# A two-layer decoder trunk on one core: the second tile's shared up projection and the shared down products move to the middle of each layer's experts, and the third pair's down weights move into two dead buffers

## The reference

```
for layer in range(2):
    mix = even_mixer(...) if layer == 0 else odd_mixer(...)
    x = layer_norm(alpha * x + mix, ln1_g, ln1_b)
    ff = moe_ffn(x, ...)          # 64 routed experts + 1 shared expert
    x = layer_norm(alpha * x + ff, ln2_g, ln2_b)
```

## Time and profile before

| what | us |
|---|---|
| median of 3 runs (1289.89 to 1291.04) | 1290.01 |
| the profiled execution's own time | 1290.57 |
| its span | 1288.8 |
| TensorE busy in it | 1216.6 |
| layer 0's first up product of the experts starts | 201.9 |
| layer 0's last combine ends | 668.2 |
| layer 1's first up product of the experts starts | 809.3 |
| core's end | 1288.8 |

### The profile page before, as it was taken

How to read it: one execution, slowest core, us unless ns; L and a number is a source line. 1 busy time by engine, 2 the same in 40 slices (tenths; PEclk the granted TensorE clock), 3 DMA queues, 4 the chain that set the end, 5 groups by cost and what they waited for, 6 DMA issues and landing times.

```text
span 1288.8 us, 16653 instructions
## 1 busy us (share of the span) xinstructions
PE 1216.6 (94%) x6664; PEld 576.4 (45%) x6664; DVE 401.3 (31%) x884; ACT 299.2 (23%) x649; POOL 27.9 (2%) x97
## 2 busy tenths in 40 slices
PE   8999999999999989899979999999999998999995
PEld 5777854334343433333336665443434333343331
DVE  3667274212121221212133646321212212121214
ACT  3354322222121211111121343121112111111112
POOL 1004000000000000000010000000000000000000
PEclk9999999999999999999989999999999999999998
DMA  9317049899999999999992646699999999999992
GB/s 369 154 34 303 1 163 392 330 395 427 429 429 427 429 430 427 428 430 426 427 382 101 261 196 248 274 358 398 427 428 429 429 428 429 428 428 429 428 427 108
DMA packets 44716, 447.42 MB, mean 347 GB/s; under 512 B 8064, under 2 KB 9472, under 8 KB 18816
## 3 DMA queue, kind: packets, MB, share of 16 engines
q1 hardware_dynamic: 44080, 446.29, 83.3%
q10 hardware_dynamic: 592, 0.53, 0.2%
HBM read 445.75 MB, written 1.05 MB: 347 GB/s over the span
## 4 chain that ended last, share of the span: by engine, by line
PE 76%; DMA 16%; DVE 5%; ACT 2%; issue 1%; DVEq 0%; SPq 0%; ACTq 0%
PE psum L404 28%; DMA w_up_ring<-in_moe_up 15%; PE psum L509 13%; PE psum L420 4%; PE psum L2246 4%; PE psum L2101 4%; PE psum L1214 3%; PE psum L490 3%; PE psum L1664 2%; PE psum L604 2%; PE psum L469 2%; PE psum L638 1%; DVE moe_h L1061 1%; PE psum L1502 1%; PE psum L2252 1%
## 5 line engine op out<-in xcount | busy, mean ns | idle before, releaser
L404 PE MATMUL psum<-w_up_ring,moe_x_selected 128*64 128x512 f32 x2048 | 454.9, 594 | 20.4 <-DMA w_up_ring<-in_moe_up 20.4
L404 PEld LDWEIGHTS psum<-w_up_ring,moe_x_selected 128*64 128x64 f32 x2048 | 149.5, 137 | 314.8 <-issue 275.8
L509 PE MATMUL psum<-w_down_ring,moe_hT 128*64 128x512 f32 x992 | 226.5, 598 | 0.0
L1061 DVE SCALAR_TENSOR_TENSOR moe_h<-moe_silu,moe_slot_gate,psum 128x256 f32<-128x256 f32 x64 | 30.7, 480 | 406.8 <-ACT moe_silu L818 406.6
L818 ACT ACTIVATE moe_silu<-psum 128x256 f32<-128x256 f32 x64 | 24.6, 384 | 446.5 <-PE psum L404 446.5
L509 PEld LDWEIGHTS psum<-w_down_ring,moe_hT 128*64 128x64 f32 x992 | 68.1, 136 | 122.8 <-issue 108.8
L1066 DVE TENSOR_TENSOR moe_out_low<-psum,moe_out_high 128x512 fp32r<-128x512 f32 x64 | 44.3, 692 | 220.2 <-ACT moe_out_high L830 220.2
L830 ACT CAST moe_out_high<-psum 128x512 fp32r<-128x512 f32 x64 | 37.4, 585 | 125.2 <-PE psum L509 125.2
L1068 DVE TENSOR_TENSOR moe_out_low<-psum,moe_out_high 128x512 fp32r<-128x512 f32 x64 | 44.3, 692 | 65.6 <-ACT moe_out_high L832 65.6
L490 PE MATMUL psum<-moe_out_high,moe_matchT 32*128 32x512 f32 x496 | 62.4, 494 | 1.8 <-DVE moe_out_low L1068 1.8
L2101 PE MATMUL psum<-w_up_ring,mixed_transposed 128*128 128x512 f32 x128 | 56.5, 593 | 0.7 <-ACT mixed_transposed L1894 0.7
(11 more groups left out here) (499 smaller groups left out, 1069.1 us busy)
## 6 DMA issues: line engine op xcount, KB each, us to landing
w_up_ring<-in_moe_up SPq DMA_DIRECT2D x128, 2048.0 KB, 20.9
w_down_ring<-in_moe_down SPq DMA_DIRECT2D x62, 2048.0 KB, 20.7
w_up_ring<-in_ev_columns SPq DMA_DIRECT2D x4, 2048.0 KB, 15.4
w_up_ring<-in_od_w_in SPq DMA_DIRECT2D x4, 2048.0 KB, 15.1
w_up_ring<-in_ev_out SPq DMA_DIRECT2D x2, 2048.0 KB, 7.7
moe_shared_weights<-in_shared_up SPq DMA_DIRECT2D x2, 2048.0 KB, 7.7
w_up_ring<-in_od_w_out SPq DMA_DIRECT2D x2, 2048.0 KB, 7.8
ln_gain_bias<-in_ln_g SPq DMA_DIRECT2D x4, 512.0 KB, 9.3
```

The source lines that it names most:

```text
L404: last = nc.tensor.matmul(k.psum[e * SLOTS:(e + 1) * SLOTS, 6, :], xsel[:, kk, own:own + SLOTS], up_view(par, e, kk), start=kk == 0, stop= ...
L509: last = nc.tensor.matmul(k.psum[e * SLOTS:(e + 1) * SLOTS, bank, :], hT[:, j * P + e * SLOTS:j * P + (e + 1) * SLOTS], places[e][:, j, ha ...
L1061: nc.vector.scalar_tensor_tensor(h[:], silu[:], slot_gate[:, i:i + 1], up_ps[:, FE:2 * FE], ALU.mult, ALU.mult).then_inc(s.h, 1)
```

## The change

For each layer:

- The shared up weights get a place of their own below `SHARED_OFFSET` (where `w_down_extra` was), so nothing overwrites them. In layer 1 they are loaded by the odd mixer's loads, where the extra down weights were.
- Tile 1's `shared_up` leaves `first_two_pairs` and stands in quad 3, ahead of pair i = 1, with its output in bank 5. The four transposes stand ahead of i = 2.
- The four pieces of `shared_down` leave quad 7 and stand in quad 4, one ahead of each pair.
- Quads 3 and 4 are written out, between two loops (quads 1 and 2, quads 5 and 6).
- Pair 2's down weights go, in two loads of 1 MB, into `k.ln` (behind the norm) and `k.x` (behind the transposes and the low part). The ln2 tables are loaded later, behind pair 2's down product, and `k.x` is rebuilt by two additions on VectorE ahead of quad 7.

The diff, cut to its core:

```diff
@@ -44,6 +44,7 @@
+SHARED_UP, SHARED_DOWN = 3, 4
@@ -325,7 +326,7 @@
-    shared_w = at("shared_weights", [P, 2, KD, FE], F32, SHARED_OFFSET)
+    shared_w = mixer.shared_w if layer else at("shared_weights", [P, 2, KD, FE], F32, SHARED_OFFSET - 8 * KF * D)
@@ -364,12 +365,16 @@
-    extra_down_both = mixer.extra_down if layer else at("w_down_extra", [P, 2, KF, D], F32, SHARED_OFFSET - 8 * KF * D)
-    extra_down = [extra_down_both[:, i] for i in range(2)]
+    third_down = [k.ln[:], k.x[:]]
...
+    shared_bank = (1, 5)
+
+    def peeled(q, quad):
+
+        return isinstance(q, int) and q == quad
@@ -519,23 +524,23 @@
     def sync(sp):
         mixer.sync(sp)
         mixer.over(sp)
-        sp.dma_start(shared_w[:].rearrange("p a k f -> p (a k f)"), d.shared_up[layer]).then_inc(s.shared_w, 16)
+        if layer == 0:
+            sp.dma_start(shared_w[:].rearrange("p a k f -> p (a k f)"), d.shared_up[layer]).then_inc(s.shared_w, 16)
...
         sp.wait_ge(s.normed1, NT)
-        for i, src in enumerate((d.ln2_g, d.ln2_b)):
-            sp.dma_start(k.ln[:, i, :], src[layer:layer + 1].to_broadcast([P, D])).then_inc(s.tables, 16)
+        load_down(sp, third_down[0], d, layer, 2, 0, x.dn_norm)
+        sp.wait_ge(s.xT_psum, 2 * NT)
+        sp.wait_ge(s.parts, NT)
+        load_down(sp, third_down[1], d, layer, 2, 1, x.dn_tokens)
...
-        if layer == 0:
-            load_down_pair(sp, extra_down_both[:], d, layer, 2, x.dn_extra)
...
         refill_down(3, 1, 1, 2)
         refill_up(4, 2, 0)
+        sp.wait_ge(s.down_b, 3)
+        for i, src in enumerate((d.ln2_g, d.ln2_b)):
+            sp.dma_start(k.ln[:, i, :], src[layer:layer + 1].to_broadcast([P, D])).then_inc(s.tables, 16)
         refill_up(5, 2, 1)
@@ -648,19 +656,13 @@
             pe_up(1, 1, 16).then_inc(s.up, 1)
-            shared_up(1, range(KD)).then_inc(s.shared_up, 1)
             pe_turn_match().then_inc(s.match_turned, 1)
...
-            pe.wait_ge(s.shared_h, NT)
+            pe.wait_ge(s.shared_h, 1)
             pe.wait_ge(s.h, 2)
-            for t in range(NT):
-                for j in range(KF):
-                    last = nc.tensor.transpose(k.psum[:, 6, (t * KF + j) * P:(t * KF + j + 1) * P],
-                                               sh[:, t, j * P:(j + 1) * P], k.ident[:])
-            last.then_inc(s.shared_hT_psum, 1)
@@ -681,7 +690,15 @@
-            if final:
+            if peeled(q, SHARED_UP) and i == 1:
+                pe.wait_ge(s.matchT, q + 1)
+                shared_up(1, range(KD)).then_inc(s.shared_up, 1)
+            if peeled(q, SHARED_UP) and i == 2:
+                shared_turn()
+            if peeled(q, SHARED_UP) and i == 3:
+                pe.wait_ge(s.shared_hT, 1)
+                pe.wait_ge(s.shared_wd, 16)
+            if peeled(q, SHARED_DOWN):
                 shared_down(i // 2, i % 2)
             pe.wait_ge(s.h, p)
@@ -717,10 +735,15 @@
-        with pe.Fori(1, QUADS - 1) as q:
+        with pe.Fori(1, SHARED_UP) as q:
             for i in range(4):
                 pair(q, i)
-        pe.wait_ge(s.shared_wd, 16)
+        for q in (SHARED_UP, SHARED_DOWN):
+            for i in range(4):
+                pair(q, i)
+        with pe.Fori(SHARED_DOWN + 1, QUADS - 1) as q:
+            for i in range(4):
+                pair(q, i)
@@ -1085,16 +1120,23 @@
+        dve.wait_ge(s.down_b, 3)
+        for t in range(NT):
+            step(nc.vector.tensor_tensor(k.x[:, t, :], x_high[:, t].rearrange("p k c -> p (k c)"),
+                                         x_low[:, t].rearrange("p k c -> p (k c)"), ALU.add))
         for i in range(4):
             pair(QUADS - 1, i, final=True)
@@ -2229,7 +2271,7 @@
         load_down_pair(sp, k.w_down_both[:, 2:4], d, 1, 1, x.dn1)
-        load_down_pair(sp, extra_down[:], d, 1, 2, x.dn_extra)
+        sp.dma_start(shared_w[:].rearrange("p a k f -> p (a k f)"), d.shared_up[1]).then_inc(moe.shared_w, 16)
```

More of the change, by code:

```diff
@@ L252 @@
 EXPERT_SEMAPHORES = dict(
-    experts="router gu0a gu0b gu1a gu1b dn0 dn1 dn_extra",
+    experts="router gu0a gu0b gu1a gu1b dn0 dn1 dn_norm dn_tokens",
     moe="mixed variance1 root1 normed1 tables shared_w shared_wd xT_psum xT dve x_high parts logits scores selected places "
@@ L603, in shared_up @@
             for kk in rows:
-                last = nc.tensor.matmul(k.psum[:, 1 + t, :], k.xT[:, kk, t * P:(t + 1) * P], shared_w[:, :, kk, :],
+                last = nc.tensor.matmul(k.psum[:, shared_bank[t], :], k.xT[:, kk, t * P:(t + 1) * P], shared_w[:, :, kk, :],
                                         start=kk == 0, stop=kk == KD - 1)
@@ L674, in first_two_pairs, with shared_turn @@
             pe_down(k.w_down[2:4], 1, 7).then_inc(s.down_b, 1)
-            pe.wait_ge(s.shared_hT, 1)
+        def shared_turn():
+            pe.wait_ge(s.shared_h, NT)
+            for t in range(NT):
+                for j in range(KF):
+                    last = nc.tensor.transpose(k.psum[:, 5, (t * KF + j) * P:(t * KF + j + 1) * P], sh[:, t, j * P:(j + 1) * P],
+                                               k.ident[:])
+            last.then_inc(s.shared_hT_psum, 1)
         def pair(q, i, first=False, final=False):
@@ L835, in pair @@
             p = 4 * q + i
+            if peeled(q, SHARED_UP) and i == 1:
+                shared_silu(1)
             take_silu(p)
@@ L860, in scalar @@
             pair(0, i)
-        with act.Fori(1, QUADS - 1) as q:
+        with act.Fori(1, SHARED_UP) as q:
+            for i in range(4):
+                pair(q, i)
+        for q in (SHARED_UP, SHARED_DOWN):
+            for i in range(4):
+                pair(q, i)
+        with act.Fori(SHARED_DOWN + 1, QUADS - 1) as q:
             for i in range(4):
@@ L1071, in pair @@
             p = 4 * q + i
+            if peeled(q, SHARED_UP) and i == 1:
+                shared_h(1)
+            if peeled(q, SHARED_UP) and i == 2:
+                dve.wait_ge(s.shared_hT_psum, 1)
+                nc.vector.tensor_copy(shT[:].rearrange("p t j c -> p (t j c)"), k.psum[:, 5, :]).then_inc(s.shared_hT, 1)
             gated_h(q, i)
@@ L1094, in vector @@
             pair(0, i)
-        with dve.Fori(1, QUADS - 1) as q:
+        with dve.Fori(1, SHARED_UP) as q:
             for i in range(4):
                 pair(q, i)
+        for q in (SHARED_UP, SHARED_DOWN):
+            for i in range(4):
+                pair(q, i)
+        with dve.Fori(SHARED_DOWN + 1, QUADS - 1) as q:
+            for i in range(4):
+                pair(q, i)
+        dve.wait_ge(s.down_b, 3)
+        for t in range(NT):
+            step(nc.vector.tensor_tensor(k.x[:, t, :], x_high[:, t].rearrange("p k c -> p (k c)"),
+                                         x_low[:, t].rearrange("p k c -> p (k c)"), ALU.add))
         for i in range(4):
@@ L2184, in odd_mixer @@
     at_qk = SHARED_OFFSET + 16 * C
-    extra_down = again("w_down_extra", [P, 2, KF, D], SHARED_OFFSET - 8 * KF * D)
+    shared_w = again("shared_weights", [P, 2, KD, FE], SHARED_OFFSET - 8 * KF * D)
     qT, kT = again("qT", [P, WH // 2, S], at_qk), again("kT", [P, WKV, 2, S], at_qk + 8 * C)
```

15 lines of the change are left out of this document (6 added, 9 removed).

## The result

The change takes the median from 1290.53 us (1289.89 to 1291.50, 4 runs) to **1275.84 us** (1275.08 to 1277.91, 4 runs): ratio 0.9888, 95% interval 0.9875 to 0.99. The forecast was 1268.3 us. The profiled executions took 1290.57 and 1275.08 us (spans 1288.8 and 1273.4), 15.5 us apart where 22.0 were expected.

A forecast was written before the change was run, and what follows sets the result against it. The later of TensorE's readiness and the weights' landing at pair 31 was taken to set each layer's end. 2 x 11.0 = 22.0 us off gave 1268.6 or 1268.0 by starting point, forecast 1268.3 us, range 1266 to 1276.

The forecast's parts named there:

- The first pairs: Pairs 0 and 1: without tile 1's shared up product TensorE's later work comes 7.0 us earlier; moving the transposes gives nothing.
- The stream's lead: Expert weight loads through pair 6 and on: they land 6.8 us earlier a layer, taken between 6.1 and 7.4.
- Quads 3 and 4: TensorE takes on the moved shared work, 8.0 and 8.2 us, runs 7.8 then 12 us late, and stops waiting for weights.
- the starving rival: Quads 4 and 5: late TensorE lets the load queue run dry, 3 us a layer, 1274.3 us; chance 0.10.
- Pair 31: Last pair's second half: TensorE ready at 644.4 us, weights at 645.0 instead of a start at 656.0; 11.0 us off.
- the starving case: Load queue dry in quads 4 and 5: each us of DMA rest is a us at the layer's end; chance 0.10.
- A rule against it: Loop branches: priced at nothing from the rows, though a rule says branches outside the loaded window stall; 15 us by it.
- The third rival: Code: one stall of 3.8 us at each of the second loop's two branches, 15 us less gain, 1283.5 us; chance 0.03.
- The clock rival: TensorE, 450 us a layer without a wait: the clock falls to its lower level, up to 1298 us; chance 0.03.
- The odd mixer: Entry behind layer 0: first weights come 6.8 us earlier, their use 11.0; cost 0, at worst 1 us once.

The follow-up runs named there:

- one_loop: The changed kernel with one rolled loop over quads 1 to 6, the moved work of quads 3 and 4 in branches on its counter: 1272.55 us, ratio 0.9857.
- rolled_up: one_loop with the shared down pieces back in the last quad: 1278.94 us, ratio 0.9912.
- rolled_filled: one_loop with four identity transposes (results unused) in TensorE's 1.5 us wait between pairs 0 and 1: 1271.62 us, ratio 0.9853.
- rolled_23: one_loop with the up product in quad 2 and the down pieces in quad 3 instead of 3 and 4: 1277.10 us, ratio 0.9892.
- late_q7: The changed kernel with 36 identity transposes (results unused) ahead of pair 28's up product: 1276.88 us.
- code_only: The kernel before with its loop split and quads 3 and 4 written out, no work moved: 1293.57 us, ratio 1.0025.

## Why the prediction came out 7.5 us too low

- **The first pairs:** right. The up product is gone there, the match matrix comes 7.0 us earlier counted from the first up product, and the transposes gave nothing.
- **The stream's lead:** right in kind, too large. Pair 6's second half landed at 278.51 us, against 277.4 to 278.7 forecast; counted from the layer's first up product it is 6.0 us earlier in layer 0, and 4.9 in layer 1, where the low clock cost 1.7. The text left open whether the 1.3 us of the earlier trace rows would repeat, with 6.1 us if so, and took the middle. They did: the last step of pair 5's down load came 1.3 us behind the other 15, behind a block. Without the written out code the lead at pair 31 is 5.5 and 6.6 us (one_loop), 5.7 and 6.3 (rolled_up), 6.0 and 5.7 (rolled_filled): 5.9 on the mean, where the term was 6.8. Twice the difference is 1.7 us.
- **Quads 3 and 4, and the starving rival:** right. TensorE doesn't wait for weights from 278 us to pair 30. The shortest time from issue to landing is 10.5 us in layer 0 and 11.4 in layer 1, at a DMA share of 1.00 to 1.01 (8.8 forecast). rolled_23 shows that the limit is where the text put it: at 7.6 us the loads stand alone and time is lost.
- **Pair 31:** the forecast had TensorE ready at 644.4 and the weights at 645.0 us. TensorE could have started near 643.2 (3.5 us to spare by late_q7), and the weights came at 646.7. Each us of the stream is a us of the layer, as the text had it for the starving case.
- **The step that failed** is "A rule against it": "from 310 to 600 us no instruction block is read at all ... So I give branches nothing." The branches do cost nothing, 0.3 us for all of them. But the row was read as evidence on branches alone. It shows a kernel that runs six quads of one loop without a block; the change adds two written out quads and a second loop, and so eight blocks in the one stretch that can't hide them. The sum has no term for them. The third rival looked for their price on TensorE, as stalls of 3.8 us at a border, 15 us in all. They are paid in the load queue, which is full, by one DMA engine's step falling behind the rest: 1.6 and 1.4 us at pair 31 in code_only, 3.3 us in all, and 3.3 us back in one_loop.
- **The clock rival** was about long busy stretches, in both layers. What came was a drop behind a 1.5 us wait, 1.7 us once, in some executions. The wait of 0.92 us in the earlier trace rows was there before, with the transposes ahead of it; the text priced their removal at nothing and didn't ask what the longer gap does.
- **The odd mixer:** the entry cost was put at 0, at worst 1 us. The border is 1.1 us longer in the profile of the changed kernel. It is 153.2 to 153.6 us in the six kernels without written out quads (before among them) and 153.5 to 155.0 in the eight with them, so most of it seems to go with the code too. It isn't the clock: between the layers, before and the changed kernel both spend 13.7 us at the lower level. What makes the difference was not tested.

The account: 22.0 - 3.3 (code) - 1.7 (lead) = 17.0 us, against 15.5 in the profiled executions, with 1.7 us of clock in that profile. One_loop, without the first term, gains 20.0 us in the profiled execution and 18.0 in the median, and rolled_filled 18.8 in the median, against 22.0 - 1.7 = 20.3. The last us or two of the medians stay open: they lie within the spread of single executions (1270.57 to 1273.39 us in one_loop).

## What to carry to other kernels

Where the DMA queue never rests and the end waits for its last load, everything else that the DMA engines do can come on the critical path, instruction blocks included: look at the instruction queues in the stretch that is full, not at the average over the span, and count written out loop bodies there at a us or two rather than at nothing (two bodies cost 1.6 us a layer here, six about 2). Here work that is wanted in one iteration alone was cheaper in a branch on the loop's counter than in a peeled copy. And a wait that is emptied by a move may cost more than it had hidden: in 4 of 14 places here the clock fell behind it.

## What the runs showed that was not expected

- Code costs in one direction only: splitting a loop with identical work made the kernel 3.3 us slower, with no gap of TensorE's own; with all six quads written out it was 4.1 us, not clearly more.
- A block of 16 KB took 1.02 to 1.11 us of one DMA engine and set that engine's step back by 1.4 to 1.7 us in every later load of a full queue. The landing moves only when that engine was among the latest: mostly at one or two blocks in eight, by 0.5 to 1.7 us.
- Moving 1 MB of tables out of the queue made pair 6's weights 2.3 and 1.4 us earlier and the kernel only 0.7 us faster: by pair 31 most of the lead was gone, in layer 0 1.0 us of it to one block.
- A branch not taken cost TensorE some 0.01 us.
- The granted clock fell to its lower level behind a wait of 1.5 us in 4 of 14 places (0.52 over a stretch of 3.4 us in the changed kernel), and with 0.66 us of transposes in that wait in none of 14.
